# Reordering VectorE's work in a two-part hybrid model kernel, and moving its mask conversions to ScalarE

## The reference

```
h = rmsnorm(x, norm_g);  proj = h @ w_in        # 1024 x 10256
# A: eight heads of two maps of 64 features, values of 128
q, k = rope(rmsnorm(.), cos, sin);  a = softmax(q0 k0) - lam * softmax(q1 k1)
oa = rmsnorm(a @ v) * attn_norm_g * (1 - lam_init) * silu(az);  ya = oa @ w_out_a
lam = exp(sum(lq1*lk1)) - exp(sum(lq2*lk2)) + lam_init
# B: eight heads of an mLSTM: q, k through a causal convolution of four taps and silu,
#    decays from the input gate and the running sum of log_sigmoid(forget gate)
yb = (sigmoid(bo) * rmsnorm(h_b) * silu(bz)) @ w_out_b
x = x + (sigmoid(ga) * ya + sigmoid(gb) * yb) @ w_o
```

## Time and profile before

| | |
|---|---|
| median of three runs | 3269.02 us (3268.58 to 3269.62) |
| the profiled execution: time, span | 3267.22 us, 3265.4 us |
| mean granted clock of TensorE | 0.990 of 2.4 GHz |
| busy: PE, PEld, DVE, ACT, POOL | 97%, 81%, 48%, 26%, 63% |
| first block | layer 1 to about 738 us, layer 2 to about 1447 us |
| loop over heads | 56.7 to 285.1 us and 760.3 to 993.2 us, seven turns each |
| ScalarE's queue at the start | 13 transfers issued from 0.75 to 7.6 us |

### The profile page before, as it was taken

One profiled execution on the slowest core, in us unless ns is written; L12 is line 12 of the kernel. 1 busy time (PEld: TensorE's weight loads), 2 busy tenths in 40 slices (PEclk: granted clock), 3 DMA queues, 4 the chain that ended last, 5 costly groups with the idle time before them and its releaser, 6 DMA issues.

```text
span 3265.4 us, 48785 instructions
## 1 busy us (share of the span) xinstructions
PE 3183.5 (97%) x15234; PEld 2653.9 (81%) x15234; DVE 1571.5 (48%) x2527; ACT 840.3 (26%) x1737; POOL 2057.7 (63%) x2052
## 2 busy tenths in 40 slices
PE   6999999999999999999999999999999999999998
PEld 5787888887787888888888888888888888888886
DVE  7777673246776762246665223112266662231122
ACT  4545532014554340022222002102122220021021
POOL 5555566775455657776656776666665657776664
PEclk9999999999999999999999999999999999999999
DMA  3222222232222222232222222222322222222222
GB/s 114 71 90 78 78 96 90 96 100 79 77 83 72 96 80 95 96 117 87 81 87 71 96 96 97 97 97 97 114 81 87 78 80 97 96 97 97 97 97 84
DMA packets 91057, 295.45 MB, mean 90 GB/s; under 512 B 13632, under 2 KB 14528, under 8 KB 90960
## 3 DMA queue, kind: packets, MB, share of 16 engines
q1 hardware_dynamic: 75456, 271.61, 25.1%
q10 hardware_dynamic: 15504, 22.55, 2.4%
HBM read 279.40 MB, written 2.13 MB: 86 GB/s over the span
## 4 chain that ended last, share of the span: by engine, by line
PE 87%; DVE 6%; ACT 3%; issue 2%; DMA 1%; ACTq 1%; DVEq 0%; POOL 0%; SPq 0%; POOLq 0%
PE bank L577 27%; PE bank L579 27%; PE bank L578 27%; PE bank L618 2%; DVE bank L1448 1%; PE bank L657 1%; PE bank L747 1%; ACTq L1084 1%; DMA rot_k<-xk 1%; DVE xk L1535 1%; PE bank L780 1%; PE bank L729 0%; PE bank L764 0%; ACT sq_k L1100 0%; PE bank L765 0%
## 5 line engine op out<-in xcount | busy, mean ns | idle before, releaser
L561 POOL TENSOR_TENSOR w_lo<-raw,w_hi 128x512 fp32r<-128x512 f32 x1024 | 1383.4, 1351 | 85.4
L558 POOL TENSOR_SCALAR w_hi<-raw 128x512 fp32r<-128x512 f32 x1024 | 691.2, 675 | 1093.8 <-DMA raw<-in_w_in 764.0
L577 PE MATMUL bank<-h_lo,w_hi 128*128 128x512 f32 x2816 | 1120.0, 398 | 1.9 <-DVE h_lo L1469 0.7
L579 PE MATMUL bank<-h_hi,w_hi 128*128 128x512 f32 x2816 | 1105.6, 393 | 0.0
L578 PE MATMUL bank<-h_hi,w_lo 128*128 128x512 f32 x2816 | 1105.0, 392 | 0.0
L577 PEld LDWEIGHTS bank<-h_lo,w_hi 128*128 128x128 f32 x2816 | 534.4, 190 | 116.2 <-issue 2.7
L579 PEld LDWEIGHTS bank<-h_hi,w_hi 128*128 128x128 f32 x2816 | 533.9, 190 | 113.9
L578 PEld LDWEIGHTS bank<-h_hi,w_lo 128*128 128x128 f32 x2816 | 534.1, 190 | 109.5 <-issue 1.7
L1448 DVE TENSOR_TENSOR bank<-bank,r_b 128x512 f32<-128x512 f32 x272 | 189.6, 697 | 380.1 <-PE bank L579 370.9
L1464 DVE TENSOR_TENSOR x<-x,bank 128x512 f32<-128x512 f32 x64 | 44.0, 687 | 332.8 <-PE bank L579 332.1
L577 PE MATMUL bank<-up_lo,w_hi 128*128 128x512 f32 x512 | 199.2, 389 | 0.0
(11 more groups left out here) (296 smaller groups left out, 4300.5 us busy)
## 6 DMA issues: line engine op xcount, KB each, us to landing
raw<-in_w_in SPq DMA_DIRECT2D x288, 512.0 KB, 3.3
raw<-in_w_up SPq DMA_DIRECT2D x64, 512.0 KB, 3.3
raw<-in_w_down SPq DMA_DIRECT2D x64, 512.0 KB, 3.3
raw<-in_w_out_a SPq DMA_DIRECT2D x16, 512.0 KB, 3.3
raw<-in_w_out_b SPq DMA_DIRECT2D x16, 512.0 KB, 3.3
raw<-in_w_o SPq DMA_DIRECT2D x16, 512.0 KB, 3.3
raw<-in_p_ret SPq DMA_DIRECT2D x16, 512.0 KB, 3.3
raw<-in_p_sb SPq DMA_DIRECT2D x16, 512.0 KB, 3.3
```

The lines of the kernel that those rows point to most:

```text
L558: nc.gpsimd.tensor_scalar(m.w_hi[:, slot, w], m.raw[:, slot, w], 1.0, 0.0, ALU.mult, ALU.add).then_inc(s["w_step"], 1)
L561: nc.gpsimd.tensor_tensor(m.w_lo[:, slot, w], m.raw[:, slot, w], m.w_hi[:, slot, w].bitcast(F32), ALU.subtract).then_inc(s["split"], 1)
L577: nc.tensor.matmul(dst, hi, rhs_lo, start=first, stop=False, **more)
L579: return nc.tensor.matmul(dst, hi, rhs_hi, start=False, stop=last, **more)
```

## The change

VectorE's order is changed in three places, and work is moved between two engines. (1) In the turn of the heads `scaled()` of the values' accumulator stands ahead of `rotated(1, 1)`. (2) `gate_rows` is cut in two: `forget_logarithms` (its wait and its first two operations), then `scaled()`, then the rest. (3) `lambdas` is cut in four: `lambda_sums` stays where it was, at the start and at the end of a layer; `gate_weights_high`, `gate_weights_low` and the rest go into the start of the layer, between the first scalings and cosines. (4) Four of the five masks are converted by ScalarE, behind its sine tables, and the fifth, `ident_b`, is dropped; the counts of `masks_ready` follow. (5) The transfer of `ident` is issued ahead of those of the gain and of four tiles of x.

```diff
@@ TensorE
-                pe.wait_ge(s["masks_ready"], 6)
+                pe.wait_ge(s["masks_ready"], 5)
@@ ScalarE, norm_of_input and the transfers
                 sine_tables()
                 log_exp_tables()
+                act.wait_ge(s["mask_in"], 16)
+                for dst, src in ((m.grp_r, C_GRP), (m.mq_b, C_MQ), (m.mx_b, C_MX)):
+                    activation(dst[:], m.cst[:, src:src + P], ACT.Copy).then_inc(s["masks_ready"], 1)
+                activation(m.ms_b[:], m.cst[:, C_MS:C_MS + TB * P], ACT.Copy).then_inc(s["masks_ready"], 1)
...
+            act.dma_start(m.ident[:], cst[:, C_IDENT:C_IDENT + P]).then_inc(s["ident_in"], 16)
             gain_load(t["gain_0"][0])
             for n in range(1, KT, 2):
                 act.dma_start(m.x[:, n], t["x"][n]).then_inc(x_in[n], 16)
-            act.dma_start(m.ident[:], cst[:, C_IDENT:C_IDENT + P]).then_inc(s["ident_in"], 16)
@@ VectorE
-            def lambdas():
+            def lambda_sums():
...
+            def gate_weights_high():
+                own(ts(m.wif_hi[:], m.wif[:], 1.0, None, ALU.mult))
+
+            def gate_weights_low():
+                tt(m.wif_lo[:], m.wif[:], m.wif_hi[:].bitcast(F32), ALU.subtract).then_inc(s["wif_ready"], 1)
+
+            def lambdas():
...
-                own(ts(m.wif_hi[:], m.wif[:], 1.0, None, ALU.mult))
-                tt(m.wif_lo[:], m.wif[:], m.wif_hi[:].bitcast(F32), ALU.subtract).then_inc(s["wif_ready"], 1)
...
-            def gate_rows():
+            def forget_logarithms():
                 dve.wait_ge(s["row_ln_ready"], at.at("layer", 1))
                 own(ts(m.fcum[:], m.frow[:], 0.0, None, ALU.min))
                 own(tt(m.fcum[:], m.fcum[:], m.lrow[:], ALU.subtract))
+
+            def gate_rows():
...
-            lambdas()
-            dve.wait_ge(s["mask_in"], 16)
-            dve.wait_ge(s["ident_in"], 16)
-            for dst, src in ((m.ident_b, m.ident[:]), (m.mq_b, m.cst[:, C_MQ:C_MQ + P]),
-                             (m.ms_b, m.cst[:, C_MS:C_MS + TB * P]), (m.mx_b, m.cst[:, C_MX:C_MX + P])):
-                nc.vector.tensor_copy(dst[:], src).then_inc(s["masks_ready"], 1)
-            ts(m.grp_r[:], m.cst[:, C_GRP:C_GRP + P], 1.0, None, ALU.mult).then_inc(s["masks_ready"], 1)
-            dve.wait_ge(s["masks_ready"], 6)
+            lambda_sums()
+            dve.wait_ge(s["masks_ready"], 5)
...
-                cosines(1, 0, 1, scaled())
+                c = scaled()
+                gate_weights_high()
+                cosines(1, 0, 1, c)
                 key_squares_low(0)
-                cosines(0, 0, 2, scaled())
+                c = scaled()
+                gate_weights_low()
+                cosines(0, 0, 2, c)
+                lambdas()
                 rotated(1, 0)
...
                     key_squares_low(1)
+                    scaled()
                     rotated(1, 1)
-                    scaled()
                     keys_split(1, 2)
...
+                forget_logarithms()
+                scaled()
                 gate_rows()
-                scaled()
                 head_normalised()
...
-                lambdas()
+                lambda_sums()
                 add_and_norm(1)
```

More of the change, by code:

```diff
@@ L248, in __init__ @@
         self.col = place.put("col", [P, 40])
-        self.ident_b = place.put("ident_b", [P, P], BF16)
         self.mq_b = place.put("mq_b", [P, P], BF16)
```

## The result

The changed kernel takes 3212.53 us (median of 4 runs, 3209.74 to 3213.2), the kernel before 3268.8 (4 runs, 3265.59 to 3269.62): a ratio of 0.9828, 95% interval 0.9811 to 0.9845. The profiled execution took 3212.89 us with a span of 3211.1, and the mean granted clock is 0.996 in place of 0.990. The forecast was 3214.

The account below looks back on a forecast made before the run. PE, busy 97% of the span, was taken as the bound, losing time only to waits and lower-clock stretches behind them. Gains 38.1 + 6.7 + 10.1 - 0.3 = 54.6 from the 3269.0 median gave 3214, range 3208 to 3229.

Parts of the forecast that it names:

- A: Heads' loop, 14 turns: values scaled before the key rotation removes 25.7 of waits and 12.4 of clock loss, 38.1 us.
- turns of 29.8 to 29.9: Sign in the heads' loop: with the wait gone, turns last 29.8 to 29.9 us at clock 1.00.
- B: First layer's start: scaling at 30.15 in place of 36.36, scores at 50.0 in place of 56.7; gain 6.7 us.
- C: Gate rows behind the values, once per layer: the o_sb waits go, gain 11.1 less 1.0, so 10.1 us.
- D: Second layer's start: lambdas operations moved there from the layer's end cost 0.3 us.
- The 1.0 that I set against it: Loss after the moved gate rows: accumulators of the first pair wait behind VectorE, 0.5 us per layer.
- E: Kernel start: issuing ident earlier gains nothing, as PE still waits for the sum of squares; loss at most 0.5 us.
- Rival 1: Heads' loop: low squares become late in most turns, 12 x 1.27 = 15 us, so 3228; chance 0.12.
- Rival 2: The clock is lost all the same without the waits; gain only 37 us, so 3232; chance 0.05.
- rival 3: The loop's wait hangs on the keys' group sum, not the copy before it, and stays; 3252; chance 0.03.
- Rival 4: Slower: VectorE's own chain in a turn grows to 34.6 us beside POOL's splitting; 3276; chance 0.02.

Follow-up runs that it names:

- roots_first: Kernel before with ScalarE's Ln and Exp for the keys moved ahead of the copy of vT; 3243.5 us, ratio 0.9934.
- the masks alone: Kernel before with masks converted by ScalarE and ident_b dropped, lambdas whole in its old place; 3265.64 us in one run.
- start_only: Kernel after with the moves of the values' scaling and of the gate rows undone; 3262.43 us, ratio 0.9994 to the kernel before.
- C alone: Kernel before with only the gate rows' scans moved behind the values' scaling; 3257.18 us, ratio 0.9976.
- a_only: Kernel before with only the values' scaling moved ahead of the key rotation; 3225.6 us, ratio 0.9885.
- best_a: Kernel after with ScalarE's key roots ahead of the rot_q transfers at the layer's start and lambdas behind the queries' split; 3211.61 us, ratio 0.9819.
- fill_wait: Kernel before with eight unread 512-column products filling PE's wait between the products with the values and the transposes; 3254.62 us, ratio 0.9965.
- best_ab: best_a with the keys' low squares moved ahead of the queries' split in the turn of the heads; 3216.4 us, ratio 0.9835.

## Why the prediction was right

**A** was to give 38.1 and gave 40.1 in the span. Its steps hold one by one: the scaling starts within 0.1 of the panel's end in steady turns, the wait is gone in all 14 turns, nothing is late in its place but sqk_lo now and then (3.4 us in three waits in the whole kernel). The waits are 25.7 of the gain. The rest, 14.4, was put at 12.4, all of it clock, and that split is off. The turns themselves show it: before, a turn with the wait at clock 1.00 lasts 31.79, with 1.95 of waiting in it, and after 29.64, so it had 0.2 more than the wait that is listed. The sign "turns of 29.8 to 29.9" missed by the same 0.2, and `roots_first` repeats it (31.03 with 1.19 of waiting). Over 14 turns that is 2.8, a term which the sum lacked, and it leaves about 11.6 for the clock. Why a wait costs 0.2 more than its row says is not shown; PE's busy time of a product is modelled (0.39 at a spacing of 0.23), which would hide about that much at each stop.

**B** was to give 6.7 and gave 5.7: scores at 51.0 in place of 50.0. The mechanism is as stated, q_lo included (waits of 1.92 and 2.08). Of the 1.0, 0.7 is the later scaling (30.86 for 30.15), which comes from the other pattern of the additions of squares beside GpSimd, and 0.3 the way from there to the scores. The part of the term that hangs on the cut of `lambdas` was small: the masks alone bring 5.2 in one profile. And the 5.7 holds for this pair of profiles; kernels with the old start show 54.0 to 56.7, and the start alone, by medians, is worth 3.4.

**C and D** were to give 10.1 - 0.3 = 9.8 and gave 8.5; C alone, by medians, 8.7. The o_sb wait went as worked out. PE stays at 1.00 in the window where the earlier trace rows show 0.88. VectorE, then PE in after behind the loop:

```profile
285.03 1.66 DVE L1518 TENSOR_TENSOR fcum<-fcum,lrow 8x512 f32<-8x512 f32 x1
287.01 0.70 DVE L1451 TENSOR_TENSOR bank<-bank,r_b 128x512 f32<-128x512 f32 x1 [0.33 <-PE bank L578]
292.39 0.69 DVE L1604 TENSOR_TENSOR o_sb<-bank,sm 128x512 f32<-128x512 f32 x1
...
294.51 0.60 PE L617 MATMUL bank<-ident,o_sb 128*128 128x128 f32 x4
304.31 0.65 PE L617 MATMUL bank<-ident,vTb 128*128 128x128 f32 x4 [0.37 <-ACTq L1018]
```

The scaling follows the logarithms with 0.33 of waiting for the panel, o_sb is ready at 293.1, and PE comes for it at 294.5. The 1.0 that I set against it is partly the wait for the copy of vTb (0.37 and 0.6), a place that I hadn't named. Waits for hs rose from 2.8 to 5.1, but they are 5.2 in `a_only` and 6.6 in `start_only`, where C isn't made, so C doesn't explain them; what does is open. That the whole comes to 54.3 of span for a forecast of 54.6 is in part luck: A gave 2.0 more than its term, B 1.0 and C with D 1.3 less.

**E** is nothing, as foretold: the wait of 11.8 became one of 8.8 for the angles, and the sum of squares still ends the stretch. **The rivals.** Rival 1 didn't happen: late low squares came in none to two turns of a layer in after, its repeat, `a_only` and `best_a`, where the sum had kept one. Rival 2 falls with `fill_wait` and the turns of 29.64, rival 3 with `roots_first`. Rival 4's place is VectorE's chain; its busy time in a turn of after is 24.0 of 29.65, so it had the room that the forecast gave it, but `best_ab` shows that one more slow operation ahead of the scaling brings its mechanism back at a tenth of its price.

## What to carry to other kernels

When the bound engine waits for a bank or buffer, follow the releaser back through each engine's list to the first instruction that could have run earlier; here a VectorE operation, the scaling, whose input was ready stood behind one that waited for a transfer. Price a repeated wait by the turns of equal work with and without it, the clock included, as it can cost nearly twice its length, and shortening it may already save the clock. Here, with the bound engine at 99%, moving more work on the others gained nothing in three attempts, and profiles of unchanged code differed by 1 to 3 us in a stage, so look at several executions before crediting an edit with a us.

## What was not expected of the hardware

- The dose of the clock loss: in the same place of the turn, waits of 1.95 to 2.3 us were followed by a stretch at the lower level in eight of twelve turns before, at about 1.65 us each, while the two of 0.75 there and all 14 of 1.0 to 1.5 in `roots_first` were not. The Trainium skill ("TensorE: Matmul & The Clock Gate", A second HAM failure mode: psum-queue depth-cycling) tells of a kernel whose TensorE stands for short times between groups of products and so moves between both levels; the turns of before agree, those of `roots_first` show that it needn't be so.
- VectorE's addition of two 128x512 tiles took 1.63 us where GpSimd was at a subtraction as it started and 0.98 where GpSimd was at a conversion, in all 14 profiles; which of the two it met changed between kernels whose starts differ by a us or less.
- The odd long turn (31.2 for 29.64) comes in none, one or two places of a layer, also in two executions of the same code: after had them in turns 1 and 5 of layer 1, its repeat in turns 3 and 5. The slow scores behind q_lo are such a case too: waits of 1.9 to 2.1 stood ahead of both first turns in either run, and those turns took 31.18 and 31.16 in after, where the clock is 0.57 and 0.62 in their first 4 us, and 29.65 and 29.64 in its repeat, where it is 1.00.
